# Other orders in the opening and in a LayerNorm, and two heads' share of an output tile formed early, in a one-core diffusion backbone step

## The reference, cut to what matters

```python
m = silu(cond) @ w_mod[l] + b_mod[l]                    # six rows of 1024 for context, six for latents
h = rms_norm(x, norm_mix[l]) * (1.0 + sc1) + sh1
# layer 0: cq = rms_norm(h @ w_dq); q = rms_norm(cq @ w_uq); ckv = rms_norm(h @ w_dkv); k, v = ckv @ w_ukv
o  = softmax(q k^T * scale) @ v                         # per head; context sees context, latents see all 768 keys
x  = x + g1 * (o_of_all_heads @ w_o)
# layer 1: y = depthwise_conv(glu(h @ w_pw1)) + b_dw;  y = silu(layer_norm(y)) @ w_pw2 + b_pw2
x  = x + g1 * y
x  = x + g2 * (silu(h2 @ w_gate) * (h2 @ w_up)) @ w_down
```

## Time and profile before

| | us |
|---|---|
| median of 3 runs (lowest, highest) | 1634.05 (1632.44, 1634.27) |
| the profiled execution | 1635.48 |
| its span | 1633.7 |
| PE busy in the span | 1599.7 |
| DVE, ACT, POOL busy | 922.9, 666.2, 287.6 |

### The profile page before, as it was taken

How to read it: one execution, slowest core, us unless ns; L and a number is a source line. 1 busy time by engine, 2 the same in 40 slices (tenths; PEclk the granted TensorE clock), 3 DMA queues, 4 the chain that set the end, 5 groups by cost and what they waited for, 6 DMA issues and landing times.

```text
span 1633.7 us, 26252 instructions
## 1 busy us (share of the span) xinstructions
PE 1599.7 (98%) x11123; PEld 1553.6 (95%) x11123; DVE 922.9 (56%) x1541; ACT 666.2 (41%) x1000; POOL 287.6 (18%) x344
## 2 busy tenths in 40 slices
PE   7999999999999999999999999989999999999998
PEld 5889889899999999999999999979999999999998
DVE  5556766766766544554367989987742323223232
ACT  3445545553544423432245656674532212211122
POOL 0011111000165524452342122330000000000000
PEclk9999999999999999999999999999999999999999
DMA  9322332132354434433333298873132122222211
GB/s 321 100 79 85 106 99 78 35 117 78 98 168 139 152 117 138 142 127 123 118 121 98 62 192 162 181 143 101 65 98 76 61 77 78 78 78 72 77 59 65
DMA packets 142381, 178.12 MB, mean 109 GB/s; under 512 B 12945, under 2 KB 121177, under 8 KB 141240
## 3 DMA queue, kind: packets, MB, share of 16 engines
q1 hardware_dynamic: 120048, 109.68, 21.2%
q0 software_dynamic: 21888, 66.66, 16.4%
q10 hardware_dynamic: 328, 0.10, 0.0%
HBM read 148.93 MB, written 2.79 MB: 93 GB/s over the span
## 4 chain that ended last, share of the span: by engine, by line
PE 83%; DVE 9%; DMA 4%; ACT 2%; issue 1%; SPq 1%; POOL 0%; DVEq 0%; ACTq 0%; POOLq 0%
PE PS L699 26%; PE PS L701 25%; PE PS L704 25%; DVE YACC L2350 4%; DMA ZACC<-ZTAP 2%; PE PS L769 1%; PE PS L1041 1%; PE PS L796 1%; PE PS L1052 1%; DMA MODS<-in_w_mod 1%; DMA Y<-SHIFT 1%; PE PS L1004 1%; DVE GP L2314 0%; DVE HL L1930 0%; PE PS L985 0%
## 5 line engine op out<-in xcount | busy, mean ns | idle before, releaser
L699 PE MATMUL PS<-HH,WH 128*128 128x320 f32 x1776 | 410.7, 313 | 8.2 <-DVE HL L1930 7.7
L701 PE MATMUL PS<-HL,WH 128*128 128x320 f32 x1776 | 405.0, 309 | 0.0
L704 PE MATMUL PS<-HH,WL 128*128 128x320 f32 x1776 | 403.8, 309 | 0.0
L1775 DVE TENSOR_TENSOR WL<-RAW,WH 128x2048 fp32r<-128x2048 f32 (+2 forms) x87 | 196.4, 2257 | 203.2 <-ACT WH L1313 203.1
L699 PEld LDWEIGHTS PS<-HH,WH 128*128 128x128 f32 x1776 | 296.0, 188 | 10.2 <-issue 7.2
L701 PEld LDWEIGHTS PS<-HL,WH 128*128 128x128 f32 x1776 | 298.4, 188 | 0.0
L704 PEld LDWEIGHTS PS<-HH,WL 128*128 128x128 f32 x1776 | 298.2, 189 | 0.0
L1313 ACT ACTIVATE WH<-RAW 128x2048 fp32r<-128x2048 f32 (+2 forms) x95 | 171.5, 1805 | 111.3 <-PE PS L704 111.3
L1946 DVE SCALAR_TENSOR_TENSOR X<-PS,MODV,X 128x128 f32<-128x128 f32 (+2 forms) x192 | 72.4, 433 | 198.8 <-PE PS L704 198.7
L621 POOL TENSOR_TENSOR BGACC<-BGACC,BGW 128x512 f32<-128x512 f32 x98 | 135.0, 1378 | 194.9 <-ACT BGW L1569 193.8
L699 PE MATMUL PS<-HIDH,WH 128*128 128x320 f32 x704 | 162.2, 311 | 0.7 <-DVE HIDL L2273 0.7
(11 more groups left out here) (329 smaller groups left out, 2268.4 us busy)
## 6 DMA issues: line engine op xcount, KB each, us to landing
BGW<-in_w_mod POOLq DMA_DIRECT2D x112, 256.0 KB, 3.0
RAW<-in_ffn_w_gate SPq DMA_DIRECT2D x22, 1024.0 KB, 5.3
RAW<-in_ffn_w_up SPq DMA_DIRECT2D x22, 1024.0 KB, 5.3
RAW<-in_ffn_w_down SPq DMA_DIRECT2D x16, 1024.0 KB, 5.1
MODA<-in_w_mod POOLq DMA_DIRECT2D x48, 256.0 KB, 3.8
RAW<-in_conv_w_pw SPq DMA_DIRECT2D x16, 512.0 KB, 5.2
WL<-RAW POOLq DMA_DIRECT2D x8, 1024.0 KB, 9.8
RAW<-in_ffn_w_down SPq DMA_DIRECT2D x8, 768.0 KB, 4.4
```

Of the source, the lines that this page charges most:

```text
L699: mm(o, wh, xh, start=first, stop=False)
L701: mm(o, wh, xl, start=False, stop=False)
L704: ins = mm(o, wl, xh, start=False, stop=last)
L1775: V.tensor_tensor(WL[:, u % 2, 0:n], RAW[:, u % 2, 0:n], WH[:, u % 2, 0:n].bitcast(F32), ALU.subtract).then_inc(lo_done, 1)
```

## The change

In the opening the spread of 1/rms is issued before the last quarter of `first_rows`; ACT's copies swap in the same way. 14 dummy steps follow `turn_first`. The second half's `MODS` lies in other memory (over later attention buffers), its sums come after (0, 1) and (2, 1), its turns after (1, 1) and (3, 0) of the first pair, and ACT copies the two quarter rows after tiles 3 and 5. DVE's `apply` is split into `scale_tile` and `low_tile` (the same instructions), which for this norm alone are written out one by one.

In attention, outputs 0 and 1 are split in head 6's last part. `early_outputs` forms their part of `("wo", 0)` in a PSUM tile of its own, `wpart`, with the weights of `("wo", 0)`: head 0's before turn 3 of head 7, head 1's after it. ACT copies it to `WPART`, DVE adds it to X with the gate, and the pair leaves those two heads out for its first tile. ACT's roundings of outputs 0 to 3 no longer stand between the exponentials of head 7.

In LayerNorm the sums of tiles 6 and 7 come before those of 4 and 5, each tile's two column groups wait for that tile alone, and the first of the two runs of dummy steps has 8 instead of 12.

```diff
@@ -113,6 +113,7 @@
...
+EARLY = 2
@@ -147,7 +148,7 @@
...
-    o += [("stat", "mix0"), ("turn", "mix0"), ("mrow", 0), ("rb", "mix0"), ("mods", 0), ("mrow", 1), ("mods", 1)]
+    o += [("stat", "mix0"), ("turn", "mix0"), ("rb", "mix0"), ("mrow", 0), ("mods", 0), ("mrow", 1), ("mods", 1)]
@@ -161,7 +162,7 @@
...
-        o += [("pt", h, t) for t in range(3)]
+        o += [("pt", h, t) for t in range(3)] + ([] if more else ["wpart"])
@@ -245,10 +246,8 @@
...
-        HALF_H = KT // 2 * HW * 4
...
-                   [R_HH + HALF_H, R_HH + HALF_H + 4096, R_HL + HALF_H, R_HL + HALF_H + 4096]
-                   + [R_HID + 32768 + 4096 * i for i in range(4)]]
+                   [R_HID + 20480 + 4096 * i for i in range(7)] + [R_P + 6144]]
@@ -743,16 +743,18 @@
...
-            def pair(names, w, xh, xl, wait, between=None):
+            def pair(names, w, xh, xl, wait, between=None, done=0):
...
+                        if j == 0 and k < done:
+                            continue
...
-                                     k == 0, k == KT - 1)
+                                     k == (0 if j else done), k == KT - 1)
@@ -844,8 +846,11 @@
...
-                rows = begin(("mrow", 0))
...
+                    if k == KT - 2:
+                        spread(("rb", "mix0"), diagn, DIAGS["mix0"])
+                    if k == 0:
+                        rows = begin(("mrow", 0))
@@ -879,6 +884,7 @@
...
+                return ps
@@ -893,14 +899,17 @@
 
                 if (k, j) == (0, 1):
                     later_rows(0)
-                if (k, j) == (3, 1):
+                if (k, j) == (1, 1):
+                    turn_later(0)
+                if (k, j) == (2, 1):
                     later_rows(1)
+                if (k, j) == (3, 0):
+                    turn_later(1)
 
             turn_sums()
             pe.wait_ge(sem("sc_ready"), 2)
             first_rows()
-            spread(("rb", "mix0"), diagn, DIAGS["mix0"])
-            turn_first()
+            hold_clock(turn_first(), HOLD + 2)
 
             h_wait = lambda n: (lambda k: pe.wait_ge(sem("h_ready"), KT * n + k + 1))
 
@@ -908,10 +917,7 @@
...
-                if k == KT // 2 - 1:
-                    turn_later(0)
...
-                    turn_later(1)
@@ -1065,6 +1071,20 @@
...
+
+            def early_outputs(first, last):
+
+                s = U[("wo", 0)] % 2
+                if first == 0:
+                    low_there(pe, U[("wo", 0)])
+                    begin("wpart")
+                for k in range(first, last + 1):
+                    pe.wait_ge(sem("o_split"), k + 1)
+                    ins = split3(halves(tile2("wpart")), WH[:, s, k * 256:k * 256 + P], WL[:, s, k * 256:k * 256 + P],
+                                 [(OH[:, k, i * HALF:(i + 1) * HALF], OL[:, k, i * HALF:(i + 1) * HALF]) for i in range(2)],
+                                 k == 0, k == EARLY - 1)
+                if last == EARLY - 1:
+                    ins.then_inc(mm_done, 1)
@@ -1115,8 +1135,12 @@
...
+                if not more:
+                    early_outputs(0, 0)
...
+                    if not more and t == 3:
+                        early_outputs(1, EARLY - 1)
@@ -1134,7 +1158,7 @@
...
-                    pair([("wo", 0), ("wo", 1)], w, OH, OL, lambda k: pe.wait_ge(sem("o_split"), k + 1))
+                    pair([("wo", 0), ("wo", 1)], w, OH, OL, lambda k: pe.wait_ge(sem("o_split"), k + 1), done=EARLY)
@@ -1248,14 +1272,14 @@
...
-                if k < KT - 2:
-                    pe.wait_ge(sem("sq_made"), SQ_BASE["ln"] + k + 3)
-                else:
-                    pe.wait_ge(sem("sq_made"), SQ_BASE["ln"] + KT - 1)
-                    pe.wait_ge(sem("last_squared"), 1)
...
-                    ins = mm(rows[COLG * g:COLG * (g + 1), 0, 0:3 * P], ONES[:, 0:COLG], LNQ[k + g // 2][:, halves3[g % 2]],
-                             start=(k == 0), stop=(k == KT - 2))
+                    m = k + g // 2
+                    if m < KT - 2:
+                        pe.wait_ge(sem("sq_made"), SQ_BASE["ln"] + m + 2)
+                    elif m == KT - 1:
+                        pe.wait_ge(sem("last_squared"), 1)
+                    ins = mm(rows[COLG * g:COLG * (g + 1), 0, 0:3 * P], ONES[:, 0:COLG], LNQ[m][:, halves3[g % 2]],
+                             start=(k == 0), stop=(k == KT - 4))
@@ -1269,8 +1293,8 @@
...
-            square_sums(4)
-            square_sums(KT - 2).then_inc(mm_done, 1)
+            square_sums(KT - 2)
+            square_sums(KT - 4).then_inc(mm_done, 1)
@@ -1282,7 +1306,7 @@
...
-            hold_clock(rows, HOLD)
+            hold_clock(rows, HOLD - 4)
@@ -1390,9 +1414,9 @@
...
+            spread_copy(("rb", "mix0"), RSTD, QT)
...
-            spread_copy(("rb", "mix0"), RSTD, QT)
@@ -1401,10 +1425,10 @@
...
-                if k == 2:
+                if k == 3:
...
-                if k == 3:
+                if k == 5:
@@ -1497,6 +1521,8 @@
...
+                if k < EARLY:
+                    filled(act, ("vt", HEADS - 1))
@@ -1517,8 +1543,6 @@
...
-                    if h + 1 == HEADS and t:
-                        round_output(t - 1)
@@ -1533,8 +1557,13 @@
                         g, c0 = (t - 1) // 2, (t - 1) % 2 * P
                         A(PTH[:, g, :, c0:c0 + P], flat(tile2(n))[:, 0:5 * P].rearrange("p (k q) -> p k q", q=P),
                           ACT.Copy).then_inc(sem("pt_hi"), 1)
+                    if t == 2 and h + 2 == HEADS:
+                        round_output(0)
                     if t == 2 and h + 1 < HEADS:
                         sum_rows(h + 1)
+                    if t == 3 and h + 1 == HEADS:
+                        filled(act, "wpart")
+                        A(row2(WPART[:]), tile2("wpart")[:, :, 0:HALF], ACT.Copy).then_inc(free_of("wpart"), 1)
                 if h + 1 < HEADS:
                     rotary_high(h + 1)
                 if h < N_ROWS:
@@ -1546,8 +1575,10 @@
                     a, b = ((0, CTX), (CTX, CTX + 256), (CTX + 256, TOK))[g]
                     A(O[:, h, a:b], tile2(n)[:, 0, 0:b - a], ACT.Copy).then_inc(free_of(n), 1)
                     if h + 1 == HEADS:
-                        for k in ((4,), (5, 6), ())[g]:
+                        for k in ((2, 3), (4, 5, 6), ())[g]:
                             round_output(k)
+                    if h + 2 == HEADS and g == 0:
+                        round_output(1)
                 if h + 1 < HEADS:
                     values(h + 1)
                     spread_copy(("rk", h + 1), RK, NKT)
@@ -1996,20 +2024,32 @@
...
-            def between(k):
-
-                if k == KT // 2 - 1:
-                    dve.wait_ge(hi_done, 1)
-                    split_first(1)
-                    dve.wait_ge(sem("part_turned"), 1)
-                    first_part(("mods", 1), 0, 4, 6)
-                if k == KT // 2:
-                    filled(dve, ("mods", 1))
-                    first_part(("mods", 1), 1, 6, 8)
-
...
-            apply("mix0", 0, 0, second=between, first=low_first)
+            was_read(dve, ("rb", "mix0"))
+            scale_tile("mix0", 0, 0, 0)
+            low_first()
+            low_tile(0, 0, 0, 0)
+            scale_tile("mix0", 0, 0, 1)
+            scale_tile("mix0", 0, 0, 2)
+            low_tile(0, 0, 1, 1)
+            scale_tile("mix0", 0, 0, 3)
+            low_tile(0, 0, 2, 1)
+            low_tile(0, 0, 3, 0)
+            dve.wait_ge(hi_done, 1)
+            split_first(1)
+            dve.wait_ge(sem("part_turned"), 1)
+            first_part(("mods", 1), 0, 4, 6)
+            scale_tile("mix0", 0, 0, 4)
+            scale_tile("mix0", 0, 0, 5)
+            low_tile(0, 0, 4, 1)
+            low_tile(0, 0, 5, 0)
+            filled(dve, ("mods", 1))
+            first_part(("mods", 1), 1, 6, 8)
+            scale_tile("mix0", 0, 0, 6)
+            scale_tile("mix0", 0, 0, 7)
+            low_tile(0, 0, 6, 1)
+            low_tile(0, 0, 7, 0)
@@ -2196,17 +2236,26 @@
...
+                    if t == 2 and h + 2 == HEADS:
+                        split_output(0)
...
+                    if h + 2 == HEADS:
+                        split_output(1)
...
-                    for k in range(HEADS - 1):
+                    for k in range(EARLY, HEADS - 1):
...
+            was_read(dve, "wpart")
+            for a, b, s in SEGS:
+                ins = V.scalar_tensor_tensor(out=X[:, 0, a:b], in0=WPART[:, a:b], scalar=MODV[:, 0, s, 16:17], in1=X[:, 0, a:b],
+                                             op0=ALU.mult, op1=ALU.add)
+            link(ins)
...
@@ -1903,38 +1934,35 @@
...
+            def scale_tile(norm_name, l, half, k):
...
+            def low_tile(l, half, k, ahead):
...
```

More of the change, by code:

```diff
@@ L324, in program @@
         ZTAP = [sb(f"ZTAP{i}", [P, RUN], (R_T[0] + 5248, R_HID + 26048)[i]) for i in range(ACT_TAPS - 1)]
+        WPART = sb("WPART", [P, TOK], R_T[2])
         TDH = sb("TDH", [P, DIAG_SLOTS, P], R_P, F32R)
@@ L1904, in scaled_first @@
```

(53 more changed lines are left out.)

## The result

The changed kernel takes 1625.01 us (median of 4 runs, 1624.66 to 1625.45) against 1633.24 us (4 runs, 1632.29 to 1634.27: one run more than in the table above) for the kernel before on the same chip. The ratio is 0.9942 with a 95% interval of 0.9930 to 0.9955: 8.2 us between the medians. The forecast was 1625.7, from a gain of 8.3. The profiled execution of the changed kernel is one of these runs: 1624.66, span 1622.9. Against the profiled execution of before (1635.48) it is 10.8 us shorter.

A forecast was written before the change was run, and what follows sets the result against it. The prediction took PE, busy 98% of the span, as the bound, leaving its gaps and half clock to win. Opening 5.0, attention 1.9 and LayerNorm 1.4 gave 8.3, so 1625.7 us; 8-in-10 range 1623.8 to 1629.3.

The forecast's parts named there:

- (a): Opening: the spread of 1/rms goes ahead of the last quarter of rows, so the turn begins at 24.35, 0.4 gained.
- (b): Opening: DVE makes HL of tile 0 before scaling tile 1; PE starts at 29.1, 1.3 gained in all with (a).
- (d): Opening: second-half rows are summed and turned earlier, leaving one wait of 0.45 for ACT; late rows at 49.2, today 54.22.
- (c): Opening: 14 dummy steps keep PE at 2.4 GHz, so twelve matmuls take 1.75 instead of 3.47, 1.7 gained.
- Rivals 2 and 3: Opening: transfers hold it, 1628.3, chance 0.12; a second-half load lands late, each us after 38.4 costing one, chance 0.04.
- Attention, 1.9 forecast: Head 7's end: two matmul sets move between transposes; the pair is 1.75 shorter and begins at 343.4 instead of 343.54.
- both waits: Head 7's end: PE idles 1.4 before turn 3 for DVE's PTCH read, and 0.5 for ACT's partial-sum copy.
- bound of 0.5: Attention's lower bound: a fall of the clock costs 1.3 to 1.4 and would leave 0.5 of the gain.
- LayerNorm, 1.4 forecast: Sum order brings the row copy and transposes 0.65 earlier, fewer dummies let the spread begin 1.45 earlier; bounds 0.65 and 1.6.
- What PE reaches earlier it should end earlier: From 345 to 1076 and after LayerNorm PE has next to no waits, so gains carry through unless a transfer holds it.
- did no harm: Opening's single gap of 1.65 at 20.9, cited as evidence that attention's new gaps would not make the clock fall.
- best bound: Whole kernel: the gain if all terms come out best, 9.5; the 8-in-10 range was said to reach from it.

The follow-up runs named there:

- the opening alone: The kernel before with only the opening's edits, including the 14 dummy steps: 1628.07 us, ratio 0.9952.
- the dummies alone: The kernel before with nothing but the opening's 14 dummy steps after the first turn: 1633.24 us, ratio 0.9992.
- LayerNorm undone: The changed kernel with LayerNorm's edits undone, opening and attention kept: 1627.33 us, ratio 0.9952.
- after again: The changed kernel itself, run once more beside the last set of experiments: 1625.87 us, ratio 0.9941.
- both shares first: The changed kernel with both heads' shares ahead of head 7's turn 3 and the partial sum copied before turn 3's probabilities: 1623.98 us, ratio 0.9938.
- attention undone: The changed kernel with attention's edits undone, opening and LayerNorm kept: 1628.12 us, ratio 0.9954.
- both improvements: The changed kernel with both heads' shares and the partial sum's copy ahead of turn 3, plus 10 dummy steps in head 0's gaps: 1622.54 us, ratio 0.9923.
- head 0's dummies: The changed kernel with 10 dummy steps in the waits of head 0's start: 1624.96 us, ratio 0.9942.

## Why the prediction came out as it did

**The total was right, the split was not.** 8.3 was forecast, and the medians are 8.2 apart on the first chip and 9.0 on the last (1634.92 to 1625.87). That the total came out so close is in part luck: the opening gave about 1 us more than forecast, attention and the stretch behind the opening gave less. By stages:

*Opening, 5.0 forecast.* The steps (a), (b) and (d) are in the rows: first product 29.26 for 29.1, sums at 31.18 and 37.21 for 30.9 and 37, late rows 48.74 for 49.2; the turn that was to wait 0.45 for ACT has no such wait. (c) holds in seven of the eight profiled executions that have the new order and the dummies: the twelve matmuls to the first sum take 1.92 instead of 3.47, and the kernel without the dummies is 1.9 later at the late rows. In the eighth the clock fell while the dummies ran, as shown above. What was off is the base. The old opening's late rows are at 54.22, 54.55, 54.85 and 56.16 in the four profiled executions that have it whole, mean 54.9. The changed opening's are at 48.5 to 48.9 in six, at 49.4 where MODS landed late, and at 49.6 where the dummies ran at half clock. So the gain is about 6, and the profile before was the quickest of its kind. Rivals 2 and 3 (transfers hold the opening) are not seen in any profile of the new order: from the first product to head 0 no wait of PE for MODS or for a late load is among its rows.

*Attention, 1.9 forecast.* The mechanism was right in both waits, in their places and to 0.4 us in their sizes, and the clock did not fall in any of the profiled executions with the new tail. The mis-sized term is again the base. Of the 1.9, some 1.25 was the old tail's fall of the clock, which half of the profiled executions do not have. By the traces the edits are worth 1.75 - (10.17 - 9.17) = 0.75 where it does not fall, and 1.75 + (10.43 - 10.16) = 2.0 where it does. The times fit either figure and prove none: 0.8 by the ratio alone (0.9995), 2.2 when undone. The prediction took its bound of 0.5 for the case in which the *new* tail falls; the old one's not falling was never a case.

*LayerNorm, 1.4 forecast.* By the traces right: the stage takes 15.5 with the old order (the opening alone, the dummies alone, LayerNorm undone) and 14.0 with the new (after, after again, both shares first, attention undone), so 1.5; where a tile of Y landed late it is 16.4 to 16.9 with the old order (three profiles) and 15.0 with the new (two). Two profiles with the new order and no late tile lie off, 14.2 (both improvements) and 15.1 (head 0's dummies, with the wait of 0.93). The time when undone, 1.5, agrees within its noise. The 16.9 of the profile before has 1.4 more than 15.5, and with it goes one long gap, not an order. The squares wait for the tiles of Y. ACT's squares, of the kernel before and of the changed one:

```profile
1084.67 0.74 ACT L1728 ACTIVATE LNQ<-Y 128x640 f32<-128x640 f32 x1 [3.01 <-DMA Y<-SHIFT]
```
```profile
1074.68 0.74 ACT L1759 ACTIVATE LNQ<-Y 128x640 f32<-128x640 f32 x1 [0.99 <-DMA Y<-SHIFT]
```

*The step that failed.* "What PE reaches earlier it should end earlier" was claimed from gaps that were listed from 345 on; the stretch between the opening and head 7 was passed over. Head 0 has three gaps there, 2.2 us in all. In the 12 profiled executions that leave them open the clock falls in 11, for 3.4 or 6.8 us; in the two in which dummies fill them it does not fall. From the late rows to head 7, less the extra length of the `MODA` sums (0.1 to 1.55 in all), the stretch takes 276.6 without a fall (three profiles), 278.0 to 278.2 with 3.4 us of it (seven), 279.0 to 279.5 with 6.8 (four): so the short fall costs about 1.5 and the long one about 2.6. The profile of the changed kernel had the long one where that of the kernel before had the short one, and gave back 0.9 of what it had won. Whether the change makes the long fall more frequent is not shown: it is in one of the five profiles with the old opening and in three of the seven with the new one and open gaps. The error did not show in the total, because the opening gave more than forecast.

Two smaller points of the prediction do not hold as it has them. It took the gap of 1.65 at 20.9 as one that "did no harm"; in the profile of LayerNorm's edits alone, which has the same old opening, the clock fell at 22.8, right behind the same gap (1.66), and the sum of MODS there took 1.74 instead of 1.06. And the lower end of its range, 1623.8, is not its best bound: 1634.05 less 9.5 is 1624.55.

**Where the 10.8 between the two profiles comes from.** 5.5 opening, -0.9 head 0, 2.0 attention, 2.9 LayerNorm, of which 1.4 goes with the late tile of Y, and 1.3 in the convolution, which no edit touches. PE's waits from 915 to 1078 that differ come to 1.3 before (0.7 in which it waited for nothing that the profile shows, 0.6 for GPL) and 0.3 after; over all profiled executions the stage takes 153.8 to 158.1, without any order by edit. What makes it so was not found.

**Much of the scatter goes with the clock.** 58 executions of the kernel before ran beside the experiments. By their mean granted clock: 0.993 or 0.994, 23 executions, mean 1636.1 us; 0.995, 15, 1635.3; 0.996, 9, 1634.0; 0.997 or 0.998, 11, 1632.4. A thousandth of the mean is 3.3 us of the execution at half clock. The correlation of clock and time is -0.75, so over half of the variance goes with the clock and the rest with something else; late transfers such as those of `MODA` and Y may be among it. The 4 first runs of the changed kernel all have 0.997, the one with both improvements has 0.999 or 1.000. So a part of what the change brings may be that fewer places are left at which the clock falls.

The rule weighed in the prediction was that transposes do not keep the gate open. At the old end of head 7, where PE's work was transposes (from 333.58 to 338.3 in the repeat of the kernel before), the clock fell in three profiled executions of six with the same gaps, so these rows neither bear it out as a sure effect nor exclude it (the Trainium skill, TensorE: Matmul & The Clock Gate, Part 4: PE-mode transpose). With real products between the transposes it fell in none of eight, which is what the prediction took.

**Open:** what makes the convolution's length vary, and why the three runs of dummies in head 0 moved the time by nothing alone, yet on top of the other order by 0.0015 of the ratio, 2.4 us (0.9923 against 0.9938; the medians, from different chips, are 1.4 apart), where the traces have 2.5 and 2.7 up to head 7.

## What to carry to other kernels

A profile is one execution: before a sum is made against it, see for each stage that a change touches whether a fall of the clock or a late transfer in it belongs to the kernel or to that execution, and give the term a price for either. Price a tail behind whose gaps the clock falls in some executions and not in others as two cases, for the old kernel as well as for the new. Follow the whole stretch behind a gain for gaps, also where no edit is; and put work that is to fill a wait ahead of that wait, not around it (1.06 and 0.56 became 0.18 and nothing).

## What the runs showed of the hardware

**The same gaps, another clock.** Behind gaps of 0.86, 0.67 and 0.4, in the same order, the clock fell in three profiled executions of six. Behind head 0's three open gaps (0.68, 0.9 to 1.0, 0.3 to 0.9) it fell for 3.4 us in seven, for 6.8 in four, and not at all in one. No difference in PE's rows ahead of the gaps was found that goes with it.

**A packet of the instruction queue among six transfers.** The DMA view of the kernel before from 1077 to 1088, and of the changed kernel from 1070 to 1079 (queue and kind: packets, MB, share of the 16 engines):

```profile
q0 software_dynamic: 694, 1.57, 81.4%
q8 instruction: 1, 0.02, 0.5%
```
```profile
q0 software_dynamic: 626, 1.40, 87.9%
```

Of 14 profiled executions, five show one packet of the instruction queue between the first and the last square, and just these five have one gap of 2.1 to 3.0 us in which ACT waits for the next tile of Y, where the nine others have none over 1.2. Such packets come all through an execution, 88 of 16 KB, in this part of it some 13 to 23 us apart, and the six transfers take about 10: whether one falls among them is a matter of timing. That packet and gap go together is shown; that the packet is the cause was not tried.
